# First two feed-forward tiles interleaved by Strassen products, with the T sums taken straight from PSUM

## The reference, cut to what matters

```python
n = rmsnorm(h, ln1_g)                      # x: (1, 1024 tokens, 1024), float32
proj = n @ w_in                            # 1024 x 1536: pool group | RG-LRU branch | gate branch
...                                        # causal pooling mixer and RG-LRU mixer
h = h + mix @ w_out                        # 1024 x 1024
n2 = rmsnorm(h, ln2_g)
h = h + (silu(n2 @ w_gate) * (n2 @ w_up)) @ w_down      # D_FF = 2816
return rmsnorm(h, lnf_g)
```

## Time and profile before

| what | value |
|---|---|
| median of 3 runs | 896.58 us (896.5 to 896.87) |
| profiled execution, its own time | 896.3 us |
| span of the profiled execution | 894.5 us |
| PE busy | 882.7 us, 99% of the span |
| DVE, ACT, POOL busy | 613.7, 396.1, 273.6 us |
| granted PE clock, mean | 0.999 |

### The profile page before, as it was taken

The page is one execution under the profiler, slowest core; times in us unless marked ns, Lnnn a source line. Parts: engine busy times, 40 slices in busy tenths (PEclk is TensorE's granted clock), DMA queues, the critical chain, the costliest instruction groups (busy, mean ns, idle before and its releaser), DMA issues.

```text
span 894.5 us, 11037 instructions
## 1 busy us (share of the span) xinstructions
PE 882.7 (99%) x3980; PEld 725.7 (81%) x3980; DVE 613.7 (69%) x848; ACT 396.1 (44%) x654; POOL 273.6 (31%) x209
## 2 busy tenths in 40 slices
PE   7999999999999999999999999999999999999997
PEld 6877788888888888888888888888888888888886
DVE  5778996655679856556565664656638975787667
ACT  6689733533565323332233332333234444454456
POOL 0000032733345655545554555555540000000000
PEclk9999999999999999999999999999999999999999
DMA  9033011132020423223232332413239933333324
GB/s 322 9 96 93 24 48 48 47 118 71 1 72 0 150 75 130 83 95 136 88 130 74 102 130 69 156 56 121 95 107 377 398 104 96 95 96 99 101 83 188
DMA packets 94318, 98.01 MB, mean 110 GB/s; under 512 B 5764, under 2 KB 63672, under 8 KB 94264
## 3 DMA queue, kind: packets, MB, share of 16 engines
q1 hardware_dynamic: 83736, 78.16, 26.1%
q10 hardware_dynamic: 10528, 19.15, 7.1%
HBM read 70.81 MB, written 24.38 MB: 106 GB/s over the span
## 4 chain that ended last, share of the span: by engine, by line
PE 98%; DVE 1%; DMA 0%; ACT 0%; issue 0%; DVEq 0%; ACTq 0%
PE bank L2112 23%; PE bank L2113 23%; PE bank L2114 23%; PE bank L2000 5%; PE bank L2002 5%; PE bank L2001 5%; PE bank L1944 3%; PE bank L1945 3%; PE bank L1946 3%; PE bank L2021 1%; PE bank L1978 1%; PE bank L1957 1%; DMA h<-in_x 0%; PE bank L1966 0%; DVE nT_lo L1308 0%
## 5 line engine op out<-in xcount | busy, mean ns | idle before, releaser
L723 POOL TENSOR_TENSOR r_lo<-gu_raw,r_hi 128x512 fp32r<-128x512 f32 x84 | 115.7, 1378 | 83.4 <-ACT r_hi L1023 83.3
L723 POOL TENSOR_TENSOR r_lo<-wsum_S,r_hi 128x512 fp32r<-128x512 f32 x63 | 98.1, 1558 | 109.6 <-ACT r_hi L1023 109.6
L2112 PE MATMUL bank<-T_hi,r_lo 128*128 128x512 f32 x336 | 130.8, 389 | 0.0
L2114 PE MATMUL bank<-T_hi,r_hi 128*128 128x512 f32 x336 | 130.7, 389 | 0.0
L2113 PE MATMUL bank<-T_lo,r_hi 128*128 128x512 f32 x336 | 130.7, 389 | 0.0
L2113 PE MATMUL bank<-d_lo,h_hi 128*128 128x512 f32 (+1 forms) x312 | 120.5, 386 | 0.0
L2114 PE MATMUL bank<-d_hi,h_hi 128*128 128x512 f32 (+1 forms) x312 | 120.5, 386 | 0.0
L2112 PE MATMUL bank<-d_hi,h_lo 128*128 128x512 f32 (+1 forms) x312 | 120.5, 386 | 0.0
L1023 ACT CAST r_hi<-gu_raw 128x512 fp32r<-128x512 f32 x84 | 52.2, 621 | 143.6 <-PE bank L2114 143.6
L2112 PE MATMUL bank<-nT_hi,r_lo 128*128 128x512 f32 x252 | 98.0, 389 | 0.0
L2113 PE MATMUL bank<-nT_lo,r_hi 128*128 128x512 f32 x252 | 98.0, 389 | 0.0
(11 more groups left out here) (247 smaller groups left out, 1637.5 us busy)
## 6 DMA issues: line engine op xcount, KB each, us to landing
h_raw<-hid_ops ACTq DMA_DIRECT2D x72, 256.0 KB, 2.6
gu_raw<-in_w_ffn_gate SPq DMA_DIRECT2D x22, 512.0 KB, 3.7
gu_raw<-in_w_ffn_up SPq DMA_DIRECT2D x22, 512.0 KB, 4.8
hid_ops<-hid SPq DMA_DIRECT2D x44, 256.0 KB, 2.3
dn<-in_w_ffn_down SPq DMA_DIRECT2D x44, 256.0 KB, 9.8
hid_ops<-hsum_S SPq DMA_DIRECT2D x33, 256.0 KB, 2.6
w_raw<-in_w_in SPq DMA_DIRECT2D x11, 512.0 KB, 4.5
h<-in_x SPq DMA_DIRECT2D x8, 512.0 KB, 6.6
```

Source lines behind the costliest of these rows:

```text
L723: pool.tensor_tensor(lo_of(n)[:], a_block(f, name), f32(hi_of(n)[:]), ALU.subtract)\
L2112: pe.matmul(bank, s_lo, m_hi, start=(opens and j == 0), stop=False, skip_group_check=True)
L2114: ins = pe.matmul(bank, s_hi, m_hi, start=False, stop=(closes and j == n - 1), skip_group_check=True)
```

## The change

Six things change.

1. Tile 0 also uses seven products. Tiles 0 and 1 go side by side, in the order M1, M2, M3, M6, M7, M5, M4, each product for tile 0 and then tile 1. Their chains use banks of their own. M3 has banks 0 and 1 and is added by a second DVE addition. Entries, weight sums (`weight_sums(0)` and `(1)` now inside DVE's turns 2 to 5) and buffers are renumbered to match.
2. The T sums of token tiles 4 to 7 are made tile by tile, from the transposes' banks (`t_first`, `t_second`, in the turns 6 and 7 and after). ACT no longer copies half b = 0 of these tiles, and POOL no longer makes their `nT_lo_a`. B12 itself is no longer an operand.
3. `nT_lo_c` reads the bank too, and so `transposes(n)` for n = 13 to 15 waits for T3 of the tile before (b = 0) and for its `nT_lo_c` (b = 1).
4. The DVE work that follows the two tiles is reordered. `weight_sums(2)` and both `hidden2` of tiles 0 and 1 come later.
5. `project` issues high by high first, then low weights, then low inputs, with a wait for each operand of its own. In unit (1, 0) all low-weight matmuls come last. ACT and DVE move one pair of `x_hi`/`x_lo` ahead of the last squares and variance of the first norm.
6. Loads of gate/up weights move: tile 1's up half is not held back any more, tile 2 waits for entry 12 and tile 3 for entry 13. Some buffers move, and one low part of the output weights is written by three subtractions in place of two.

```diff
+            def t_first(i):
+                m = 4 + i
+                dve.wait_ge(xT_ok, 2 * (TT + m) + 1)
+                dve.wait_ge(nlo_a_ok, i + 1)
+                dve.tensor_tensor(raw[0][:, :, cols(i)], bank_of(0), raw[0][:, :, cols(i)], ALU.subtract).then_inc(t_ok, 1)
+                dve.wait_ge(raw_ok, raw_count(m, 1))
+                dve.tensor_tensor(raw[0][:, :, cols(m)], raw[1][:, :, cols(m)], bank_of(0), ALU.subtract).then_inc(t_ok, 1)
+            def t_second(i):
+                m = 4 + i
+                dve.wait_ge(n_hi_ok, norm_hi_count(m, 1))
+                dve.wait_ge(t_ok, t_count("T3", i))
+                dve.tensor_tensor(raw[1][:, :, cols(m)], bank_of(1), raw[0][:, :, cols(i)], ALU.subtract).then_inc(t_ok, 1)
+            def nT_lo_c(m):
+                dve.wait_ge(n_hi_ok, norm_hi_count(m, 1))
+                dve.tensor_tensor(nT_lo[:, KH:KT, cols(m)], bank_of(1), f32(nT_hi[:, KH:KT, cols(m)]), ALU.subtract)\
+                    .then_inc(nlo_c_ok, 1)
...
+            for m in range(TT):
+                add_projection(2 * TT + 2 * m)
+                if m >= 1:
+                    norm_rsqrt(NB + 2 + m, TT + m - 1, TT + m)
+                    normalise(TT + m - 1)
+                add_projection(2 * TT + 2 * m + 1)
+                if 2 <= m < 6:
+                    nT_lo_b(m - 2)
+                if m >= 6:
+                    t_first(m - 6)
+                second_variance(m)
+                if m >= 6:
+                    t_second(m - 6)
+                if m == 6:
+                    nT_lo_c(4)
+                if m in (2, 4):
+                    weight_sums(m // 4, ("S1",))
+                if m in (3, 5):
+                    weight_sums(m // 5, ("S4",))
+            norm_rsqrt(NB + 2 + TT, 2 * TT - 1, 2 * TT)
+            normalise(2 * TT - 1)
+            nT_lo_c(5)
+            t_first(2)
+            t_second(2)
+            nT_lo_c(6)
...
+            up_first(1)
+            second_sum(2)
+            hidden2(0)
+            hidden1(1)
+            weight_sums(2, ("S4",))
+            hidden2(1)
+            hidden_sums(0)
...                                              # f = 2: third_sum, weight_sums(3, S1), up_second
@@ def transposes(n, xs):
-                    if n > TT:
-                        pe.wait_ge(n_hi_ok, 2 * (n - 1) + b + 1)
+                    if n > TT + 4:
+                        if b == 0:
+                            pe.wait_ge(t_ok, t_count("T3", n - 1 - TT - 4))
+                        else:
+                            pe.wait_ge(nlo_c_ok, n - TT - 4)
+                    elif n > TT:
+                        pe.wait_ge(n_hi_ok, norm_hi_count(n - 1 - TT, b))
@@ def project(c, i, between=()):
+                    pe.matmul(bank, hi_[:, k], n_hi, start=(n == 0), stop=False)
                     if (c, i) == (0, 0) and n in (0, 4):
                         pe.wait_ge(w_lo_ok, 1 + n // 4)
+                    if not late:
+                        pe.matmul(bank, lo_[:, k], n_hi, start=False, stop=False)
                     if c == 0:
                         pe.wait_ge(n_lo_ok, x_count(i, k))
+                    ins = pe.matmul(bank, hi_[:, k], n_lo, start=False, stop=(not late and n == KT - 1))
@@ end of the tensor block
+            gate_up_product(0, "M1")
+            transposes(2 * TT - 2, xs2)
+            gate_up_product(1, "M1")
+            transposes(2 * TT - 1, xs2)
+            for pr in FIRST[1:]:
+                for f in range(2):
+                    gate_up_product(f, pr)
```

More of the change, by code:

```diff
@@ L106, in hymba_pool_rglru_block @@
         wo_hi[2] = wo_hi[0]
-        wo_lo3 = [at("wo_lo3_0", 192.25, [P, 2, 512], F32R), at("wo_lo3_1", 108, [P, 2, 512], F32R)]
+        wo_lo3 = at("wo_lo3", 192.25, [P, 2, 512], F32R)
+        wo_lo3_end = [at(f"wo_lo3_end{k}", 66 + 8 * k, [P, 512], F32R) for k in range(2)]
         y0_lo = at("y0_lo", 152.25, [P, GT, S], F32R)
@@ L1065, in silu1 @@
                 p = f // 2
[L1066 to L1071, removed]
+                act.wait_ge(ent_ok, done(entry(f, "M2")))
+                if f == 1:
+                    act.wait_ge(r_lo_ok, entry(1, "M3") + 1)
                 if p > 0 and f % 2 == 0:
@@ L1097, in copy_m1 @@
             def copy_m1(f):
[L1098 to L1101, removed]
+                if f == 0:
+                    act.wait_ge(sq_ok, 2 * TT)
+                elif f >= 2:
+                    act.wait_ge(hid1_ok, 1 if f == 2 else f)
+                act.wait_ge(ent_ok, done(entry(f, "M1")))
+                act.copy(m1(f)[:], chain_bank(f, 0)[:]).then_inc(m1_ok, 1)
+            hi_entry(4)
+            copy_m1(0)
+            nT_hi_part(2 * TT - 2)
+            copy_m1(1)
+            nT_hi_part(2 * TT - 1)
             hi_entry(5)
+            t_hi("T2", 0)
+            hi_entry(6)
+            t_hi("T2", 1)
             silu1(0)
-            t_hi("T2", 0)
-            t_hi("T2", 1)
             t_hi("T3", 0)
             t_hi("T3", 1)
-            hi_entry(6)
-            silu2(0)
-            copy_m1(1)
+            silu1(1)
+            hi_entry(7)
             t_hi("T1", 0)
             t_hi("T1", 1)
-            hi_entry(7)
-            hi_entry(8)
+            for n in range(8, 12):
+                hi_entry(n)
             t_hi("T4", 0)
             t_hi("T4", 1)
+            hi_entry(12)
+            hi_entry(13)
+            hi_entry(14)
+            silu2(0)
+            hi_entry(15)
+            silu2(1)
+            hi_entry(16)
+            hi_entry(17)
             def load_h(s):
@@ L1157, in split_dn @@
                 act.copy(d_hi[s % STEPS][:], dn[D_BLOCK[pr], k][:]).then_inc(d_hi_ok, 1)
-            for f in range(1, FT):
-                for pr in products(f):
+            for f in range(2, FT):
+                for pr in PRODUCTS:
                     n = entry(f, pr)
-                    if pr == "M1" and f >= 2:
+                    if pr == "M1":
                         copy_m1(f)
@@ L1764, in _, with up_second, up_first @@
-                if f == 1:
-                    weight_sums(2, ("S1",))
+                    dve.wait_ge(r_lo_ok, entry(0, "M5") + 1)
+                dve.tensor_tensor(u3(f)[:], chain_bank(f, 1)[:], m1(f)[:], ALU.add).then_inc(u3_ok, 1)
+            def up_second(f):
+                dve.wait_ge(ent_ok, done(entry(f, "M5")))
+                dve.wait_ge(u3_ok, f + 1)
+                dve.tensor_tensor(u3(f)[:], chain_bank(f, 2)[:], u3(f)[:], ALU.add).then_inc(c22_ok, 1)
+            def up_first(f):
+                dve.wait_ge(ent_ok, done(entry(f, "M4")))
+                dve.tensor_tensor(m1(f)[:], chain_bank(f, 1)[:], m1(f)[:], ALU.add).then_inc(c21_ok, 1)
@@ new lines, in gate_second @@
+            def gate_second(f):
+                dst = hid[f % 2][1][:]
+                dve.wait_ge(u2_ok, f + 1)
+                if f < 2:
+                    dve.wait_ge(ent_ok, done(entry(f, "M5")))
+                    step(dve.tensor_tensor(dst, chain_bank(f, 2)[:], u2(f)[:], ALU.add))
+                    dve.tensor_tensor(dst, product_bank(f, "M3")[:], dst, ALU.add).then_inc(c12_ok, 1)
+                else:
+                    dve.wait_ge(ent_ok, done(entry(f, "M3")))
+                    dve.wait_ge(hid_out, 16 * 5 * (f // 2))
+                    dve.tensor_tensor(dst, chain_bank(f, 2)[:], u2(f)[:], ALU.add).then_inc(c12_ok, 1)
@@ new lines, in _ @@
+            for name, g in T_HI[0:5]:
+                t_lo(name, g)
+            second_sum(0)
+            t_lo("T1", 1)
+            second_sum(1)
+            for name, g in T_HI[6:]:
+                t_lo(name, g)
+            third_sum(0)
+            third_sum(1)
+            up_second(0)
+            gate_second(0)
+            weight_sums(2, ("S1",))
+            up_second(1)
+            gate_second(1)
+            up_first(0)
+            hidden1(0)
+            up_first(1)
+            second_sum(2)
@@ L1766, in _ @@
+            hidden2(0)
[3 more added lines that the diff above has]
+            hidden_sums(0)
+            for f in range(2, FT):
+                if f > 2:
+                    second_sum(f)
+                if f == 2:
+                    third_sum(f)
+                if f + 1 < FT:
+                    weight_sums(f + 1, ("S1",))
+                if f > 2:
+                    third_sum(f)
+                up_second(f)
                 if f + 1 < FT:
@@ L2193, in _ @@
[L2193 to L2196 removed]
+                        closes(f, pr)).then_inc(ent_ok, 1)
+            gate_up_product(0, "M1")
[5 more added lines that the diff above has]
+                    gate_up_product(f, pr)
```

355 lines of the change are left out of this document (151 added, 204 removed).

## The result

The changed kernel takes 899.31 us in the median of 8 executions (898.12 to 900.59) against 896.86 (896.5 to 897.19). The ratio is 1.0028 with the 95% interval [1.0017, 1.0039], so it is slower, by 0.3%. The forecast was 897.5, and the range ended at 899.3.

A forecast was written before the change was run, and what follows sets the result against it. PE was taken as the bound, busy 882.7 of 894.5 us. Gains 2.72 + 0.75 = 3.5 against waits 0.6 + 2.7 + 1.1 = 4.4 gave plus 0.9: a median of 897.5 from 896.58, range 895.2 to 899.3 (8 in 10).

The forecast's parts named there:

- Product: Tile 0 has seven products in place of eight: 12 matmuls of 0.227 us fewer, 2.72 us gained in full.
- Head: Projection at the start: PE's waits at 14.58 and 17.60 and the slower matmuls behind them go, 0.75 us gained (0.4 to 0.8).
- (a): Transposes of token tile 5, second half: PE waits for nT_lo_c(4) at the end of DVE's turn 6, 0.6 us (0.5 to 1.2).
- (b): Transposes of token tile 6, second half: PE waits for nT_lo_c(5), behind DVE's root and normalise, 2.7 us (2.4 to 3.0).
- (c): Before M3 of tile 2: PE waits for DVE's row of 14 instructions with POOL collisions, 1.1 us (0 to 2.2).
- Costed at nothing: T sums, T3, T1 and T4 steps, POOL's and ACT's dropped work, weight loads and moved buffers: no added time.
- Rival A: DVE is further ahead or the order hides the long wait: 3.5 gained, at most 0.5 lost, 893.1 to 894.2; chance 0.12.
- the clock: PE's clock stays at 2.4 GHz throughout, though PE stands still for 2.7 us at the border; no cost counted.
- rival C: After PE's 2.7 us stillness the clock falls to 1.2 GHz, 2.72 us per product: 900.2 to 902.9; chance 0.04.

The follow-up runs named there:

- product_out: The kernel before without the 12 matmuls of one of tile 0's eight products, all other work as it was: 897.17 us against 896.8, ratio 1.0004.
- head_alone: The kernel before with only the new `project` order and the moved squares, `x_hi`, `x_lo` and variance: 896.13 us against 896.75, ratio 0.9993.
- c5_in_turn7: The changed kernel with nT_lo_c(5) moved into DVE's turn 7, ahead of the root and normalise: 897.46 us, ratio 1.001, one group.
- up_first_f2: The changed kernel with the addition that M3 of tile 2 waits for ahead of tile 3's weight sums on DVE: 898.01 us, ratio 1.0012.
- wait_alone: The kernel before, where the second half of token tile 6's transposes also waits for the last normalise: 898.82 to 899.25 and 900.57, 900.77 us, ratio 1.0034.
- wait_longer: The kernel before, where the second half of token tile 6's transposes also waits for POOL's low part, made twice: 902.99 to 904.75 us, ratio 1.0077.

## Why the prediction was wrong

- Product, 2.72 in full: it came, but not for the reason given. "PE is the bound, so it counts in full" is refuted by product_out, where the same 12 matmuls gain nothing. What keeps PE fed in the changed kernel is argued above and not shown. That this term came out right is luck.
- Head, 0.75: the two waits went, and from the first matmul on PE is 0.64 faster; head_alone shows 0.6.
- (a) 0.6: 1.2, my upper end. DVE entered turn 6 with its add_projection at 249.07 against 248.84, while PE ran 0.35 ahead (its last matmul of project_out(30) began at 250.79 against 251.13). So DVE was 0.6 late against PE, where I had reckoned 0.1 to 0.3.
- (b) 2.7: 2.6, in place, released by the instruction named. c5_in_turn7 shows that its cause is DVE's order.
- (c) 1.1: 1.6, with the three collisions predicted. The rest is small: 0.3 of gaps in DVE's row and 0.15 from the end of its addition (317.71) to PE's start. up_first_f2 removes the wait.
- Costed at nothing: no product of tiles 0 and 1 waits, for T sums, entries or loads. That was right.
- Rival A's upper end of 894.2 doesn't follow from its own terms: 896.58 - 3.5 + 0.5 is 893.6. Nothing hangs on it.
- The step that failed is the clock: "So I expect 2.4 GHz throughout", with 0.04 for rival C. The evidence I used, the end of the trace, was one draw: it showed that a stillness of that length can keep the clock, not that it always does. Half of the executions lie at 898.3 and half at 900.4. The size of the fall (2.1) is a little under my price for one product (2.7), and its chance was one half.

The ends of the other traces would have said so. In the kernel before, the clock fell at about 893.05, 4.8 us after PE's last matmul (888.01 + 0.28). In head_alone, whose end is the same code, it fell 2.0 us after it (887.71 + 0.28, and 889.98). The first two rows are of the kernel before, the other two of head_alone:

```profile
892.50:893.00 0.50, 0.00 (x0) 0.00 (x0) 0.00 (x0) 0.00 (x0) 0.00 (x0) 1.00 1.05 410
893.00:893.50 0.50, 0.00 (x0) 0.00 (x0) 0.00 (x0) 0.00 (x0) 0.00 (x0) 0.55 1.03 393
...
889.50:890.00 0.50, 0.00 (x0) 0.00 (x0) 0.36 (x3) 0.02 (x1) 0.00 (x0) 0.98 0.68 266
890.00:890.50 0.50, 0.00 (x0) 0.00 (x0) 0.43 (x3) 0.23 (x1) 0.00 (x0) 0.50 1.07 410
```

Over the 13 profiled executions that ended normally the delay runs from 2.0 to 5.1 us, so the earlier trace rows was one of the late ones.

On this the Trainium skill (TensorE: Matmul & The Clock Gate, Part 1: The HAM clock gate) says of the rise of the clock that its moment varies from run to run for the same kernel. The six kernels of the table show the like for the fall: it came in 0 of 11 executions behind 1.5 us, 14 of 29 behind 2.5 to 3.6, 5 of 5 behind 4.9.

The rest of the time lies in the terms: the lower group is 898.3 where the sum gave 897.5. The terms cover the 0.8 between them with a little to spare: (a), (c) and the head came out worse by 0.6, 0.5 and 0.1, (b) better by 0.1. The measured median of 899.31 is itself an accident, since it lies between two equally large groups: with one fall fewer among the eight it would be 898.4.

## What to carry to other kernels

When the order of one engine frees another's buffer, look at what stands ahead of the freeing instruction; here root and normalise, 2.0 us, stood ahead of it. A copy that already exists can free the buffer instead. Price a stillness of TensorE of 2.5 us or more as itself plus a chance of about one half of losing 1.5 to 2.1 us more to the clock (nothing between 1.5 and 2.5 us was run), and look at the single times: a median between two groups describes no execution. Taking work off a busy engine pays only where the next dependent result is already there.

## What was not expected of the hardware

The granted clock can fall after PE has resumed (0.8 us later in the changed kernel's profile), so that the stillness looks harmless in its own stretch (1.00 for 258 to 261). At 1.2 GHz matmuls of 512 columns started 0.43 us apart, at 2.4 GHz 0.23. The lower level lasted 3.4 us in the changed kernel and 3.4 in wait_alone. In wait_longer it lasted from 262.6 to 269.4, of which the first 1.0 was still idle, so a fall there costs more. Counted from the moment when PE stopped, the fall came after 2.3 us in wait_alone, 3.4 in the changed kernel and 4.0 in wait_longer, and 2.0 to 5.1 behind the last matmul of the kernels. What decides it between 2.5 and 3.6 us of stillness stays open.
